# Two-block transformer kernel on one core: top-key rounds of three query blocks interleaved, key and query rotations placed behind the masks

## The reference

```python
def block(args):
    qb, qib, wib, tb = args
    q_chunk = tb // CHUNK
    allowed = key_chunk[None, :] <= q_chunk[:, None]
    logits = jnp.einsum('bqhd,bsd->bqhs', qib, ki)
    score = jnp.einsum('bqhs,bqh->bqs', jax.nn.relu(logits), wib).astype(jnp.float32)
    score = jnp.where(allowed[None], score, -jnp.inf)
    _, idx = lax.top_k(score, topk)
...
    s = jnp.einsum('bqgrd,bqkgd->bqgrk', qb, k_sel).astype(jnp.float32) * (HEAD_DIM ** -0.5)
    s = jnp.where(valid[:, :, None, None, :], s, -jnp.inf)
    pr = jax.nn.softmax(s, axis=-1).astype(v.dtype)
```

## Time and profile before

| | |
|---|---|
| median of three runs | 2920.82 us (2919.22 to 2920.93) |
| profiled execution | 2922.66 us, its span 2920.8 us |
| PE, DVE, ACT, POOL busy | 90%, 38%, 29%, 42% of the span |
| mean granted clock of PE | 0.928 |
| the stretch in layer 0 of block 2 | about 1524 to 1642 us |
| the same in layer 1 | about 2236 to 2355 us |

### The profile page before, as it was taken

One profiled execution on the slowest core, in us unless ns is written; L12 is line 12 of the kernel. 1 busy time (PEld: TensorE's weight loads), 2 busy tenths in 40 slices (PEclk: granted clock), 3 DMA queues, 4 the chain that ended last, 5 costly groups with the idle time before them and its releaser, 6 DMA issues.

```text
span 2920.8 us, 30918 instructions
## 1 busy us (share of the span) xinstructions
PE 2634.2 (90%) x11550; PEld 2041.4 (70%) x11550; DVE 1116.1 (38%) x1838; ACT 841.3 (29%) x1096; POOL 1225.2 (42%) x448
## 2 busy tenths in 40 slices
PE   1599779999899779999889989999989898999997
PEld 1385558878686458887767657887867665888785
DVE  7685630018866460000148652000024955100004
ACT  1323332221323322221132343222123244322212
POOL 0332255544433235554344144555434424455443
PEclk6799889999899779999989799999999888999998
DMA  7421323247421332322232022222332111232231
GB/s 234 129 89 39 122 84 101 87 132 220 151 72 44 101 101 86 101 92 79 81 88 80 22 72 72 94 93 87 89 95 73 58 37 58 87 101 94 75 98 49
DMA packets 313578, 267.96 MB, mean 92 GB/s; under 512 B 20376, under 2 KB 306696, under 8 KB 313240
## 3 DMA queue, kind: packets, MB, share of 16 engines
q1 hardware_dynamic: 313496, 266.86, 29.4%
HBM read 264.74 MB, written 2.10 MB: 91 GB/s over the span
## 4 chain that ended last, share of the span: by engine, by line
PE 78%; DVE 12%; issue 4%; ACT 3%; POOL 2%; DMA 0%; DVEq 0%; SPq 0%; POOLq 0%; ACTq 0%
PE bank L1980 23%; PE bank L1981 23%; PE bank L1982 23%; DVE a_acc L1450 2%; DVE x L1735 1%; DVE m_sq L1487 1%; PE bank L2044 1%; POOL h_lo L1244 1%; DVE m_sq L1506 1%; PE bank L2236 1%; PE bank L2156 1%; DVE n_work L1819 1%; DVE m_sq L1733 1%; DVE n_top L1815 1%; PE bank L2125 1%
## 5 line engine op out<-in xcount | busy, mean ns | idle before, releaser
L1231 POOL TENSOR_TENSOR w_lo<-raw,w_hi 128x2048 fp32r<-128x2048 f32 (+1 forms) x216 | 914.5, 4234 | 1134.5 <-ACT w_hi L779 1103.8
L1980 PE MATMUL bank<-h_hi,w_lo 128*128 128x512 f32 (+1 forms) x2256 | 909.8, 403 | 79.3 <-POOL h_lo L1244 40.6
L1981 PE MATMUL bank<-h_lo,w_hi 128*128 128x512 f32 (+1 forms) x2256 | 893.4, 396 | 0.0
L1982 PE MATMUL bank<-h_hi,w_hi 128*128 128x512 f32 (+1 forms) x2256 | 892.7, 396 | 0.0
L1980 PEld LDWEIGHTS bank<-h_hi,w_lo 128*128 128x128 f32 (+1 forms) x2256 | 430.4, 191 | 215.7 <-issue 67.6
L779 ACT ACTIVATE w_hi<-raw 128x2048 fp32r<-128x2048 f32 (+1 forms) x216 | 377.7, 1750 | 487.1 <-PE bank L1982 456.5
L1982 PEld LDWEIGHTS bank<-h_hi,w_hi 128*128 128x128 f32 (+1 forms) x2256 | 432.0, 191 | 93.6
L1981 PEld LDWEIGHTS bank<-h_lo,w_hi 128*128 128x128 f32 (+1 forms) x2256 | 432.9, 192 | 88.5 <-issue 2.4
L1548 DVE TENSOR_TENSOR f_full<-f_act,bank 128x512 f32<-128x512 f32 x88 | 60.5, 688 | 893.6 <-PE bank L1982 893.6
L1980 PE MATMUL bank<-f_hi,w_lo 128*128 128x512 f32 x704 | 281.3, 400 | 13.3 <-POOL f_lo L1256 13.3
L1981 PE MATMUL bank<-f_lo,w_hi 128*128 128x512 f32 x704 | 280.9, 399 | 0.0
(11 more groups left out here) (284 smaller groups left out, 2492.5 us busy)
## 6 DMA issues: line engine op xcount, KB each, us to landing
raw<-in_ffn_w SPq DMA_DIRECT2D x44, 1024.0 KB
raw<-in_w_ffn_in SPq DMA_DIRECT2D x44, 1024.0 KB
raw<-in_w_in SPq DMA_DIRECT2D x34, 1024.0 KB
a_raw<-in_ada_w SPq DMA_DIRECT2D x64, 512.0 KB, 4.8
raw<-in_ffn_w SPq DMA_DIRECT2D x32, 704.0 KB
raw<-in_w_ffn_out SPq DMA_DIRECT2D x32, 704.0 KB
b_raw<-in_ada_w SPq DMA_DIRECT2D x16, 1024.0 KB, 5.0
raw<-in_w_out SPq DMA_DIRECT2D x8, 1024.0 KB
```

The costliest lines, as they stand in the source:

```text
L1231: pool.tensor_tensor(b.w_lo[p][:, 0:n], b.raw[p][:, 0:n], b.w_hi[p][:, 0:n].bitcast(F32), ALU.subtract)\
L1980: pe.matmul(out, wlo, xhi, start=start, stop=False)
L1981: pe.matmul(out, whi, xlo, start=False, stop=False)
L1982: return pe.matmul(out, whi, xhi, start=False, stop=stop)
```

## The change

Four things change, all in block 2, and no arithmetic. PE computes the index logits of block 2 right behind those of block 1, and those of block 3 ahead of unit 4. ACT takes the relus of block 2 right behind those of block 1, and those of block 3 behind the split of unit 5. `top` now takes a list of (block, round) turns: blocks 1 and 2 share four rounds, then all three blocks go through twelve, block 3 four rounds behind the others, and block 3 ends alone with four. Rotations 3 to 8 and the gate products come behind all masks; the order gate(0), gate(1) ahead of rotations 7 and 8 is kept.

```diff
@@ act_layer2
         split(j + 2)
-        relu(j - 1)
+        for i in ((1, 2), (3,))[j - 2]:
+            relu(i)
     for j in (4, 5):
         for m in range(2):
             take(j, m, b.n_u[:, 2 * (j - 4) + m, :], ACT.Gelu_apprx_tanh)
         split(j + 2)
-        if j == 4:
-            relu(3)
@@ dve_layer2
-    def top(blocks, rounds=range(TOPK // 8)):
+    def top(turns):
...
-        for n8 in rounds:
-            for i in blocks:
...
+        for i, n8 in turns:
+            score, work, eight = of(i)
+            if n8 == 0:
+                dve.wait_ge(*s.is_sum(l, 4 * i))
+
+                dve.memset(b.n_score[0:HD, i - 1, CAUSAL[i] - HD:CAUSAL[i]], FLOOR).then_inc(s.floor.up, 1)
+                lone_wait(dve, s, *s.floor(l, i))
+            else:
+                lone_wait(dve, s, *s.cut[i - 1](l, n8))
+            dve.max(eight, work if n8 else score).then_inc(s.top[i - 1].up, 1)
+        for i, n8 in turns:
+            score, work, eight = of(i)
+            lone_wait(dve, s, *s.top[i - 1](l, n8 + 1))
+            dve.match_replace(work, eight, work if n8 else score, TAKEN).then_inc(s.cut[i - 1].up, 1)
...
     index_scores(1)
-    top([1], range(0, 5))
     index_scores(2)
-    top([1], range(5, 10))
+    for n in range(4):
+        top([(1, n), (2, n)])
+    index_scores(3)
+    for n in range(4, 8):
+        top([(1, n), (2, n), (3, n - 4)])
     gating_moments()
-    top([1], range(10, TOPK // 8))
+    for n in range(8, 12):
+        top([(1, n), (2, n), (3, n - 4)])
+    gating_norm()
+    for n in range(12, TOPK // 8):
+        top([(1, n), (2, n), (3, n - 4)])
     mask(1)
-    index_scores(3)
-    top([2, 3], range(0, 4))
-    gating_norm()
-    top([2, 3], range(4, 8))
+    mask(2)
+    for n in range(12, TOPK // 8):
+        top([(3, n)])
+    mask(3)
     rope(3)
     rope(4)
-    top([2, 3], range(8, TOPK // 8))
-    gate(0)
-    mask(2)
     rope(5)
     rope(6)
+    gate(0)
     gate(1)
     rope(7)
     rope(8)
-    mask(3)
     gate(2)
     gate(3)
@@ pe_layer2
     index_logits(1)
+    index_logits(2)
     pe_unit(pe, e, lay, 3, 3, tokens=True)
-    index_logits(2)
+    index_logits(3)
     pe_unit(pe, e, lay, 4, 4)
-    index_logits(3)
     pe_unit(pe, e, lay, 5, 5)
```

## The result

The changed kernel takes 2934.93 us in the median (2931.26 to 2941.88, six runs), against 2920.88 us for the kernel before (2918.34 to 2927.62, six runs): a ratio of 1.0049 [1.0032, 1.0066], so it is **slower by 14 us**. The forecast was 2933.0 us, in 2925 to 2940. The profiled execution of the changed kernel took 2934.08 us (span 2932.2, mean granted clock 0.926), against 2922.66 us (span 2920.8, 0.928) for the kernel before.

A forecast was written before the change was run, and what follows sets the result against it. DVE's late rotations were taken to bound the stretch through PE's turn(5) and turn(7). DVE saves 6 us, but turn(5) comes 12.2 us later and scores 6.3 us later per layer: +12.6, 2933 us, range 2925 to 2940.

The forecast's parts named there:

- Sign and cause: Slower, because rotations 3 and 4 stand behind all rounds and masks; slower by more than the noise had chance 0.82.
- turn(5): PE's turn ahead of unit 8, waiting for DVE's rotation: forecast at 1603.9 in layer 0, 12.2 us later per layer.
- DVE's queue: DVE's work up to turn(5): rounds cost 49.3 us, not 55.4; the rest after block 3's scores sums to 53.95.
- The multiply: Block 3's first score multiply on DVE: held until 0.2 us behind POOL's split, at 1547.4; DVE loses 5.4 us.
- rival C: DVE's rounds of three interleave worse, 3.4 us each, 5.3 us more per layer: 2944 us; chance 0.11.
- rival B: Block 3's first multiply on DVE gets ahead of POOL, DVE 4.2 us earlier: +4.2 in sum, 2925.0 us; chance 0.10.
- turn(5) to the scores: PE's stretch through unit 8, gatings and turns: 38.3 us, scores 6.3 us later per layer; clock's part -2.5 to +1.5.
- the index logits: Block 2's score matmuls on PE ahead of unit 3: 1.56 us, 0.1 us of stall; unit 3 ends 1.6 us later.
- The sum: Both layers' later scores, 2 x 6.3 = +12.6 us, giving 2933.4 against the median, predicted as 2933 us.
- The range's low end: 2925 us for the whole kernel, said to take rival B and the favourable clock.
- the favourable clock: PE's clock rising or falling at better points in unit 8 and the gatings: up to 2.5 us less per layer.
- Covers that held: Waits off the path: ACT's second relus free, seventh raw tile's copy covered, moments ready 3 us before ACT asks.

The follow-up runs named there:

- the square of four kernels: Rotations 3, 4 before the last rounds or behind all masks; rounds as before: 2920.88, 2951.24 us; early logits and interleaved: 2905.47, 2934.93 us.
- relu3_first: Changed kernel with ACT doing block 3's relus ahead of unit 5's split: 2928.04 us, ratio 1.0027.
- filler_70: Changed kernel with 70 extra unread matmuls of 128x512 between unit 7 and turn(5): 2931.39 us, ratio 1.0026.
- before_rot_late: Kernel before with only rotations 3 to 8 and the gate products moved behind all masks: 2951.24 us, ratio 1.0114.
- early_logits_only: Kernel before with only the early index logits, relus and block 2 scores; rounds, rotations and masks untouched: 2906.69 us, ratio 0.9948.
- gatings_in_unit8: both_moves with the gatings cut in 16 pieces between unit 8's dense steps, turn(6) in the middle, DVE's order adapted: 2897.08 us, ratio 0.991.
- both_moves: Changed kernel with rotations 3 and 4 back among the rounds and block 3's relus ahead of unit 5's split: 2901.96 us, ratio 0.9931.
- the last kernel: gatings_in_unit8 with turn(7) also inside unit 8, behind its twelfth step, and DVE's order behind unit 8 changed: 2894.39 us, ratio 0.9902.

## Why the prediction was right, point by point

**Sign and cause: right.** PE's wait before turn(5) grew to 16.25 and 15.87 us (16 forecast), none is left before turn(7), and the square of four kernels shows the moved rotations as the cause.

**DVE's queue: right to the tenth.** Rounds of two, three and one: 1.71, 2.96 and 1.74 us against 1.70, 2.96 and 1.75. From the end of block 3's first multiply to turn(5) the sum said 56.5 us; it took 56.45 in layer 0 and 56.08 in layer 1. The largest difference inside it is that masks 1 and 2 took 1.9 us, where 1.5 and 0.7 for POOL were set down. The multiply went as forecast, held until 0.3 us behind POOL's end. That rules out rival C (rounds of 3.4 us) and rival B (the multiply ahead of POOL). relu3_first is B made on purpose: it was priced at 8 us below the forecast and gave 6.9 below the changed kernel.

**turn(5): exact in layer 1, 1.9 us late in layer 0.** 2316.4 was forecast for layer 1 (2304.23 + 12.2) and 2316.4 came, with the last part of DVE's queue 0.4 us shorter and what stands ahead of it 0.4 us longer than in the sum. In layer 0 it came at 1605.8 and not at 1603.9. The 1.9 us are there before the rounds of three begin: POOL's split began at 1545.23, 1.8 us behind the 1543.4 that the step gives with the drift of 0.79. The failed term is the index logits: the sum allowed them 0.1 us of stall and no loss of clock. The first 16 took 4.16 us in layer 0 with the clock down to 0.76, and 2.97 in layer 1 at 1.00; that is 1.2 of it, and unit 3 behind them took 0.4 us more.

**turn(5) to the scores: mis-sized.** The step said 38.3 us, with the clock's part free by -2.5 to +1.5; it took 35.7 and 35.6, just below the low end. turn(5), unit 8 and turn(6) took 14.5 and 14.2 us where layer 1 of before had 15.2, and the clock held for about 6 us of the gatings in place of about 3.5. relu3_first took 38.3 and 38.4 us for the same work behind a wait of 11 us, and filler_70 35.4 and 35.8 behind one of at most 0.5. So this piece costs 35.4 to 38.4 us, by where the clock rises and falls, and the length of the wait in front doesn't order it.

**The sum: right, partly by cancelling.** By the scores the loss was 5.6 and 3.6 us, 9.2 and not 12.6. The profiled span grew by 11.4 us. The other 2.2 us are drift outside the stretch: 0.8 in front of it, 4.6 between the two layers and 3.2 the other way behind the second. The largest piece is the layer norm, whose 16 matmuls ran in 9.95 us where they had 7.13 before. In layer 1 it was the other way round, so that pair cancels:

```profile
1740.83 9.95 PE L2237 MATMUL bank<-m_sq,ones 128*128 128x512 f32 x16 [1.44 <-ACT m_sq L1010]
...
2461.25 7.13 PE L2237 MATMUL bank<-m_sq,ones 128*128 128x512 f32 x16 [1.45 <-ACT m_sq L1010]
```

The same 16 matmuls took either about 7.1 or about 10 us in all of these kernels, in both layers at 10 in before_rot_late and at 7.1 in early_logits_only. Such steps of 2.8 us may be a part of the spread between runs of one kernel (10.6 us over these six); that isn't shown. By the medians the loss was 14.1 us, 1.5 above the forecast. That it came so close is in part luck, since the stretch itself lost 3.4 us less than the sum said.

**The range's low end: one step doesn't follow.** Rival B alone gives 2925.0 us; with the favourable clock, as the text says, it would be 2920. Nothing in the result hangs on it.

**Covers that held.** The seventh raw tile, ACT's wait for the relus and the moments cost nothing, as said: ACT asked for the moments at 1570.4, 2.8 us behind their end. Not seen in advance, and off the path: POOL's split of unit 9 held the sum of rotation 4, 5.13 us at 1608.41 on DVE, while PE was in unit 8.

## What to carry to other kernels

When an engine that isn't the bottleneck carries a long queue, look for the instruction in it that the bottleneck waits for, and count what the change puts in front of that one: here 6 us of DVE's rounds were saved and about 15 us a layer lost by two calls moved behind the masks. The parts of a change should be tried one by one, since the square above shows a gain of about 15 us hidden under a loss of about 30. A gain in one piece should be followed to the end of the stretch: filler_70 won 1.7 us in unit 8 and had lost it again by the scores. And when PE gets earlier, price what it meets next: gatings_in_unit8 ran into a wait on DVE of 5.24 us that both_moves hadn't shown, and 3.22 us of it were left in the last kernel.

## What the runs showed of the hardware that was not expected

- The clock can fall in a short group of small matmuls in one layer and not in the next: the same 16 index logits took 4.16 and 2.97 us in one execution. The kernel before has 8 of them in the group, and they took 1.14 us in both layers.
- The gatings' small matmuls lose the clock with PE busy throughout (0.50 in filler_70 for 22 us and in both_moves for 20, the first scores with them) and keep it (1.00 for 27 us) when three dense matmuls stand between every two pieces.
- DVE's top-key rounds are not held by POOL. In the changed kernel a round of three took its 2.96 us beside a whole split of POOL's (the timelines of DVE and POOL below), while a multiply of 512 columns beside such a split grew from 0.49 to 4.46 us.

```profile
1558.86 1.47 DVE L1812 MAX8 n_top<-n_work 128x8 f32<-128x256 f32 x3
1561.82 1.47 DVE L1812 MAX8 n_top<-n_work 128x8 f32<-128x256 f32 x3
```

```profile
1558.31 4.63 POOL L1230 TENSOR_TENSOR w_lo<-raw,w_hi 128x2048 fp32r<-128x2048 f32 x1 [8.46 <-ACT w_hi L779]
```
